# Seven products in place of eight for the last group of a feed-forward layer, on one Trainium2 core

## The reference

```
h2 = _rmsnorm(x, norm_mlp[l])
x = x + jnp.square(jax.nn.relu(h2 @ w_ff1[l])) @ w_ff2[l]
```

## Time and profile before

| | |
|---|---|
| median of 3 runs | 730.05 us |
| the profiled execution | 729.97 us |
| its span, first to last instruction | 728.2 us |
| PE busy | 722.0 us, 3460 matmuls |
| DVE busy | 520.8 us |
| ACT busy | 336.8 us |
| POOL busy | 241.6 us |

### The profile page before, as it was taken

The page is one execution under the profiler, slowest core; times in us unless marked ns, Lnnn a source line. Parts: engine busy times, 40 slices in busy tenths (PEclk is TensorE's granted clock), DMA queues, the critical chain, the costliest instruction groups (busy, mean ns, idle before and its releaser), DMA issues.

```text
span 728.2 us, 9745 instructions
## 1 busy us (share of the span) xinstructions
PE 722.0 (99%) x3460; PEld 576.6 (79%) x3460; DVE 520.8 (72%) x754; ACT 336.8 (46%) x483; POOL 241.6 (33%) x197
## 2 busy tenths in 40 slices
PE   8999999999999999999999999999999999999998
PEld 5878878787776666788889988888888888888887
DVE  6355887899886865537656569695968778695972
ACT  6244753465567777722334353534344252535320
POOL 4005225011224653003301091815436180816610
PEclk9999999999999999999999999999999999999999
DMA  9409231311111202133190225151331505131102
GB/s 322 149 15 264 83 117 58 116 58 58 58 58 30 74 16 57 59 116 115 38 338 3 75 98 175 59 173 58 116 115 51 179 0 177 53 115 58 58 16 101
DMA packets 44037, 70.62 MB, mean 97 GB/s; under 512 B 2657, under 2 KB 27489, under 8 KB 44002
## 3 DMA queue, kind: packets, MB, share of 16 engines
q1 hardware_dynamic: 44000, 70.16, 29.5%
q10 hardware_dynamic: 2, 0.00, 0.0%
HBM read 65.71 MB, written 2.10 MB: 93 GB/s over the span
## 4 chain that ended last, share of the span: by engine, by line
PE 94%; DVE 3%; ACT 1%; POOL 1%; issue 1%; DMA 0%; DVEq 0%; ACTq 0%
PE ps L1804 8%; PE ps L1803 8%; PE ps L1802 8%; PE ps L421 7%; PE ps L423 7%; PE ps L422 7%; PE ps L1830 6%; PE ps L1832 6%; PE ps L1831 6%; PE ps L414 6%; PE ps L416 5%; PE ps L415 5%; PE ps L1684 1%; PE ps L1620 1%; PE ps L1654 1%; PE ps L1716 1%
## 5 line engine op out<-in xcount | busy, mean ns | idle before, releaser
L1802 PE MATMUL ps<-b_hi,cut_hi 128*128 128x512 f32 (+1 forms) x280 | 104.1, 372 | 0.0
L1803 PE MATMUL ps<-b_lo,cut_hi 128*128 128x512 f32 (+1 forms) x280 | 103.9, 371 | 0.0
L1804 PE MATMUL ps<-b_hi,cut_lo 128*128 128x512 f32 (+1 forms) x280 | 103.9, 371 | 0.0
L421 PE MATMUL ps<-cut_hi,a_hi 128*128 128x512 f32 x224 | 90.3, 403 | 0.0
L423 PE MATMUL ps<-cut_hi,a_lo 128*128 128x512 f32 x224 | 87.7, 392 | 0.0
L422 PE MATMUL ps<-cut_lo,a_hi 128*128 128x512 f32 x224 | 87.6, 391 | 0.0
L909 ACT ACTIVATE qo_sb<-ps 128x512 f32<-128x512 f32 x32 | 19.2, 599 | 135.7 <-PE ps L1804 91.0
L631 POOL TENSOR_TENSOR a_lo<-qo_sb,a_hi 128x512 fp32r<-128x512 f32 x49 | 78.2, 1617 | 5.6 <-ACT a_hi L919 5.6
L405 DVE TENSOR_TENSOR cut_lo<-raw,cut_hi 128x2048 fp32r<-128x2048 f32 (+2 forms) x33 | 52.1, 1579 | 27.9 <-ACT cut_hi L397 27.9
L397 ACT ACTIVATE cut_hi<-raw 128x2048 fp32r<-128x2048 f32 (+2 forms) x33 | 48.5, 1468 | 31.1 <-PE ps L416 22.7
L1803 PEld LDWEIGHTS ps<-b_lo,cut_hi 128*128 128x128 f32 x280 | 52.8, 188 | 9.1
(11 more groups left out here) (199 smaller groups left out, 1665.7 us busy)
## 6 DMA issues: line engine op xcount, KB each, us to landing
raw<-in_w_ff_dram SPq DMA_DIRECT2D x32, 1024.0 KB, 5.6
raw<-in_w_in_dram SPq DMA_DIRECT2D x16, 1024.0 KB, 5.7
gates<-in_x_dram SPq DMA_DIRECT2D x8, 512.0 KB, 5.9
raw<-in_w_out_dram SPq DMA_DIRECT2D x4, 1024.0 KB, 5.0
raw<-in_w_in_dram SPq DMA_DIRECT2D x4, 512.0 KB, 7.4
raw<-in_w_branch_sb_dram SPq DMA_DIRECT2D x2, 1024.0 KB, 5.1
raw<-in_w_branch_sa_dram SPq DMA_DIRECT2D x4, 512.0 KB, 6.2
out_dram<-gates SPq DMA_DIRECT2D x7, 256.0 KB, 2.0
```

The source lines that it names most:

```text
L421: nc.tensor.matmul(dst, l_hi, w_hi, start=start, stop=False)
L1802: T.matmul(dst, w_hi[:, w], b_hi[:, k, a:b], start=(k == 0), stop=False)
L1803: T.matmul(dst, w_hi[:, w], b_lo[:, k, a:b], start=False, stop=False)
L1804: mm = T.matmul(dst, w_lo[:, w], b_hi[:, k, a:b], start=False, stop=(k == KD - 1))
```

## The change

Group 7 gets the seven products as well. The last full round (round 6) and group 7 are written out: PE takes the four first-product tiles of group 7 sooner, in the order tile 0, A11, S2, tile 1, A12, tile 2, S1, tile 3, S3, S4, A22; then the products of group 7 as A11, S2, S1, A12, S3, S4, A22. The second token tile of the last A22 is done in two halves of 256 columns, the second half in bank 6, and S3's part of it is added by itself. ACT, DVE and POOL get new lists to match (`act_last_end`, `dve_late`, `dve_last`, `left_parts_last`); DVE takes the first weights' second half remainder ahead of the first square. SP sends nine output parts out as `drain` finishes them.

```diff
+PE_TURN = {FG - 2: [A11, S2, A12, S1, S3, S4, A22], FG - 1: [A11, S2, S1, A12, S3, S4, A22]}
+LEFT_TURN = {FG - 1: [A11, A12, S2, S1, S3, S4, A22]}
+RIGHT_TURN = {FG - 1: PE_TURN[FG - 1]}
+OUT_PARTS = [(A12, 0, 0), (A12, 1, 0), (S3, 0, 0), (S3, 1, 0), (S4, 0, 0), (S4, 1, 0), (A22, 0, 0),
+             (A22, 1, 0), (A22, 1, 1)]
...
+        late_home = {(FG - 2, A22): home4[0], (FG - 1, A11): home4[1], (FG - 1, S2): home3[1], (FG - 1, S1): home4[2],
+                     (FG - 1, A12): home4[3], (FG - 1, S3): home3[0], (FG - 1, S4): home3[2], (FG - 1, A22): home4[0]}
...
-                sp.wait_ge(x_final, v + 1)
+                sp.wait_ge(drained, prod_end(FG - 1, q) - 1 + t + hf)
...
-            for c in range(4):
-                pool.wait_ge(hid_hi, c + 1)
-                pool.tensor_tensor(left_lo[:, c], pair(hid[:, c, :]), left_hi[:, c].bitcast(F32), ALU.subtract).then_inc(hid_lo, 1)
+            def left_parts_last(g):
+                pool.wait_ge(l_lo, 7 * g)
+                pool.wait_ge(s_made, 4 * g)
+                pool.wait_ge(f1_sq, 4 * g + 3)
+                left_low(g, A11)
+                pool.tensor_tensor(sum_of[S3], h11, h21, ALU.subtract).then_inc(s_made, 1)
+                pool.wait_ge(f1_sq, 4 * g + 4)
+                pool.tensor_tensor(sum_of[S1], h21, h22, ALU.add).then_inc(s_made, 1)
+                pool.wait_ge(s_made, 4 * g + 2)
+                pool.tensor_tensor(sum_of[S2], sum_of[S1], h11, ALU.subtract).then_inc(s_made, 1)
+                left_low(g, A12)
+                left_low(g, S2)
+                left_low(g, S1)
+                pool.wait_ge(s_made, 4 * g + 3)
+                pool.tensor_tensor(sum_of[S4], h12, sum_of[S2], ALU.subtract).then_inc(s_made, 1)
+                for q in (S3, S4, A22):
+                    left_low(g, q)
...
             def act_last_end(g):
-                last_high(0)
-                hidden_high(1)
                 right_high(g, S3)
+                right_high(g, A22)
+                right_high(g + 1, A11)
                 relu(g + 1, 2)
-                last_high(1)
-                last_high(2)
-                hidden_high(2)
-                right_high(g, A22)
-                last_high(3)
+                left_high(g + 1, A11)
+                right_high(g + 1, S2)
                 relu(g + 1, 3)
-                hidden_high(3)
+                right_high(g + 1, S1)
+                for q in (A12, S1, S2):
+                    left_high(g + 1, q)
+                right_high(g + 1, A12)
+                left_high(g + 1, S3)
+                right_high(g + 1, S3)
+                right_high(g + 1, S4)
+                left_high(g + 1, S4)
+                left_high(g + 1, A22)
+                right_high(g + 1, A22)
...
+                        if last and q == S3 and t == 1:
+                            dve.wait_ge(z_added, 6)
+                            half = xres[:, 3, 256:512]
+                            V.tensor_tensor(half, src[:, 256:512], half, ALU.add)
+                        if last and q == A22 and t == 1:
+                            V.tensor_tensor(part[:, 0:256], src[:, 0:256], part[:, 0:256], ALU.add).then_inc(drained, 1)
+                            dve.wait_ge(prod_done, prod_end(g, q) + 1)
+                            dve.wait_ge(drained, prod_end(g, S3))
+                            src, part = bank(6, 256, 512), part[:, 256:512]
...
+            def dve_late(g):
+                right_low(g, S2)
+                right_low(g, A12)
+                f_low(g + 1, 1)
+                square(g + 1, 0)
+                drain(g, A11)
+                drain(g, S2)
+                right_low(g, S1)
+                t4_made(g)
+                right_low(g, S4)
+                square(g + 1, 1)
+                drain(g, A12)
+                right_low(g, S3)
+                right_low(g, A22)
+                t1_made(g + 1)
+                right_low(g + 1, A11)
+                square(g + 1, 2)
+                t3_made(g + 1)
+                t2_made(g + 1)
+                drain(g, S1)
+                right_low(g + 1, S2)
+                square(g + 1, 3)
+                drain(g, S3)
+                right_low(g + 1, S1)
+                drain(g, S4)
+                right_low(g + 1, A12)
+                t4_made(g + 1)
+                right_low(g + 1, S3)
+                drain(g, A22)
+                right_low(g + 1, S4)
+            def dve_last(g):
+                drain(g, A11)
+                right_low(g, A22)
+                drain(g, S2)
+                add_z(S1)
+                drain(g, S1, last=True)
+                add_z(S4)
+                drain(g, A12)
+                add_z(A22)
+                drain(g, S3, last=True)
+                drain(g, S4, last=True)
+                drain(g, A22, last=True)
...
-            with pe.Fori(1, FG - 1) as g:
+            with pe.Fori(1, FG - 2) as g:
                 pe_round(g)
...
+            g = FG - 2
+            ff1(g + 1, 0)
+            product(g, A11)
+            product(g, S2)
+            ff1(g + 1, 1)
+            product(g, A12)
+            ff1(g + 1, 2)
+            product(g, S1)
+            ff1(g + 1, 3)
+            for q in (S3, S4, A22):
+                product(g, q)
+            for q in PE_TURN[g + 1]:
+                product(g + 1, q, halves=(q == A22))
```

More of the change, by code:

```diff
@@ L62, with place @@
 HI = [A11, A12, S1, S2, S3, S4, A22]
-LAST_BANK = [0, 1, 4, 5, 6, 7, 2, 3, 0]
-OUT_PARTS = [(u % TB, 512 * (u // TB), 512 * (u // TB) + 512) for u in range(7)] + [(3, 512, 768), (3, 768, 1024)]
+PE_TURN = {FG - 2: [A11, S2, A12, S1, S3, S4, A22], FG - 1: [A11, S2, S1, A12, S3, S4, A22]}
+LEFT_TURN = {FG - 1: [A11, A12, S2, S1, S3, S4, A22]}
+RIGHT_TURN = {FG - 1: PE_TURN[FG - 1]}
+def place(turns, g, q):
+    return turns[g].index(q) if isinstance(g, int) and g in turns else q
+OUT_PARTS = [(A12, 0, 0), (A12, 1, 0), (S3, 0, 0), (S3, 1, 0), (S4, 0, 0), (S4, 1, 0), (A22, 0, 0),
+             (A22, 1, 0), (A22, 1, 1)]
+PART = {A12: (0, 0), S1: (2, 1), S4: (0, 1), S3: (2, 1), A22: (2, 0)}
 ZCOL = [0, 512, 1024, 896]
@@ L381, in prod_end @@
         def prod_end(g, q):
[L383 removed]
+            return 14 * g + 2 * place(PE_TURN, g, q) + 2
         def cut_slot(i, part, k, nk):
@@ L932, in right_high @@
                     act.wait_ge(f1_done, 2)
+                elif isinstance(g, int) and (g, q) in ((FG - 2, A22), (FG - 1, A11)):
+                    act.wait_ge(f1_done, 4 * (FG - 1) + 2)
+                elif isinstance(g, int) and (g, q) in ((FG - 1, S1), (FG - 1, A12)):
+                    act.wait_ge(f1_done, 4 * (FG - 1) + 4)
+                elif isinstance(g, int) and g == FG - 1:
+                    act.wait_ge(prod_done, prod_end(FG - 2, {S2: S1, S3: S3, S4: S4, A22: A22}[q]))
                 elif not (first and q == S2):
@@ L1379, in drain @@
                     dve.wait_ge(prod_done, prod_end(g, q) - 1 + t)
-                    if last and q == A22:
-                        dve.wait_ge(z_added, 4 + t + 1)
+                    if last and q in Z_TURN:
+                        dve.wait_ge(z_added, 2 * Z_TURN.index(q) + t + 1)
                     elif not (first and back):
-                        dve.wait_ge(drained, 14 * (g + back) + 2 * wrote + t + 1)
+                        dve.wait_ge(drained, prod_end(g + back, wrote) - 1 + t)
                     src = bank(BANK[q] + t)
@@ L1825, in product @@
                     if not (first and back):
[L1826 to L1833, removed]
+                        pe.wait_ge(drained, prod_end(g + back, before) - 1 + t)
+                    for a, b in ((0, 256), (256, S)) if halves and t else ((0, S),):
+                        for j in range(2):
+                            l_h, l_l = (part[:, q, j, t * P:(t + 1) * P] for part in (left_hi, left_lo))
+                            dst = bank(6 if a else BANK[q] + t, a, b)
+                            T.matmul(dst, l_h, hi[:, j, a:b], start=(opens or a > 0) and j == 0, stop=False, skip_group_check=True)
+                            T.matmul(dst, l_h, lo[:, j, a:b], start=False, stop=False, skip_group_check=True)
+                            mm = T.matmul(dst, l_l, hi[:, j, a:b], start=False, stop=(j == 1), skip_group_check=True)
+                        mm.then_inc(prod_done, 1)
             pe.wait_ge(f_lo, 1)
@@ L1864, in _ @@
             pe_round(0, first=True)
-            with pe.Fori(1, FG - 1) as g:
+            with pe.Fori(1, FG - 2) as g:
                 pe_round(g)
[L1867 to L1887, removed]
-                mm.then_inc(last_done, 1)
+            g = FG - 2
[11 more added lines that the diff above has]
+                product(g + 1, q, halves=(q == A22))
 _INS = ["x", "norm_mix", "w_in", "q_norm_sb", "k_norm_sb", "q_norm_sa", "k_norm_sa",
```

90 lines of the change are left out of this document (30 added, 60 removed).

## The result

The changed kernel takes 731.76 us (median of 11 executions, 730.76 to 732.46); the kernel before took 730.05 beside it (11 executions, 729.76 to 730.27). The ratio is 1.0022, with a 95% interval of 1.0014 to 1.0031: slower by 1.71 us, 0.23%. That lies inside the predicted range and 0.26 us beyond the border of 731.5 between "same" and "slower"; the interval, 0.14% to 0.31%, reaches to both sides of that border (0.2%).

What follows compares the result with a forecast made beforehand. The prediction took PE's number of matmuls to bound the end. Its terms, -2.80 (matmuls) + 3.76 (stall) + 0 (outputs) = +0.96 us, on 729.97 profiled, plus 0.08 for the median, gave 731.0 us, range 728.8 to 732.9.

Steps and rivals of the forecast that it cites:

- border of 731.5: Whole kernel: 728.6 and 731.5 us bound "same"; chances were faster 0.19, same 0.51, slower 0.30.
- Part 1: PE's matmuls of group 7: 19.12 us instead of 21.92, 2.80 us less on the path.
- the relu of tile 1: Round 6: it waits for POOL's last remainder of group 6, forecast to end at 683.4 instead of 680.27.
- Part 2: Work added off PE: DVE's late A22 drain stalls PE ahead of product S2 of group 7, costing 3.76 us.
- I count four times 1.0 to 1.2: DVE's waits for POOL between 698.4 and 709.2: four, 4.45 us in all, with none to five possible.
- the sign of being right: PE gapless from 662.78 to 706.3, then one idle time of 3 to 4 us ahead of group 7's S2.
- No further wait arises: After the stall PE's banks are drained in time, 0.7 us ahead at the closest (S3 before A22).
- Part 3: ACT copies, weight load and nine closer outputs at no price: 0, up to +0.5 or -0.3 us for outputs.
- The estimate of 380 GB/s: Full output transfer rate, giving 0.7 us per 256 KB; the last 128 KB finds the queue just empty.
- rival D: Something late and unseen, such as PE's longer straight program or a slow output queue: +1 to +2 us; chance 0.03.
- Rival B: No PE stall ahead of S2 of group 7, as DVE's A22 drain comes earlier: 727.3 us; chance 0.17.
- Rival C: The stall drops PE's clock to 1.2 GHz for 3.7 us, costing 1.8 us: 732.8 us; chance 0.10.

Runs made afterwards that it cites:

- e2: The changed kernel with POOL's four sums and seven remainders of group 7 cut to 32 of 256 columns: 727.10 us.
- e4: The changed kernel with every other output transfer issued by ACT instead of SP: 731.70 us.
- e1: The changed kernel with DVE's drains of A22 of round 6 moved ahead of T4 and the remainder of S3: 730.74 us.
- e9: e5 with 200 already fulfilled waits spread over PE's program of round 6: 727.77 us.
- e10: The changed kernel with 200 already fulfilled waits in PE's program of round 6 and nothing else: 730.06 us.
- e3: The changed kernel without its first four output transfers (A12 and S3): 729.87 us.
- e6: e5 with the drain of A22 of round 6 late again, behind the remainder of S3: 732.16 us.
- e8: e5 with every other output issued by ACT: 728.93 us.
- e5: The changed kernel with six zsum additions moved from DVE to POOL, the early A22 drain of e1 and DVE's last list reordered: 729.06 us.
- e7: e1 with every other output issued by ACT: 730.83 us.

## Why the prediction was right or wrong

The time (731.0 against 731.76) and the place of the stall were right, but the middle of the sum was right only because two wrong terms nearly cancel, the stall 1.20 us too long and the outputs 1.56 too short: that is luck. And the median lies by a hair beyond the border to "slower", where "same" was the likeliest.

- **Part 1, -2.80 us: right.** e2 gives 2.80 to the hundredth. Round 6 stayed gapless in its new order; the relu of tile 1, forecast at 683.4 for POOL's last remainder, came at 683.76 with 0.34 of it the shifted start. That order wasn't tried by itself.
- **Part 2, the stall: place, releaser and mechanism right; its size, 3.76, was 1.2 too much.** The term that failed is "I count four times 1.0 to 1.2", with the reason that like rows "hold one full turn per instruction". Three turns were lost, not four, so that PE's idle time was 2.33 us, below the 3 to 4 given as the sign of being right. DVE was behind its S4 drains (PSUM, not held by POOL) at 702.71, and POOL's operation, let go at about 701.5, needs 1.25 us, thus until about 702.75, by this working: who comes first was a matter of 0.05 us, and the remainder of A12 went first, in 1.21. In e4 another remainder, that of A22, took 2.34 us where after has 1.21. Rows can show that turns are taken, not who gets each one; the range for this (none to five) held, the point estimate deserved less weight.
- **"No further wait arises": right for after,** with a margin given as 0.7 us. e1 shows how thin it was: with the first wait cured the gap stands at that very bank, 1.64 us.
- **Part 3, outputs, "0" with a bound of +0.5: wrong, +1.56.** The estimate of 380 GB/s was right (376 GB/s from 726 to 728), and so was the queue just emptying, but for something that isn't an output: the fetch of PE's longer straight program. The prediction named "the longer straight PE program" only in rival D, at 0.03; D's price, +1 to +2, is what came. The packet was to be seen in the trace of before, in the queue of instructions at 700 to 702; I read the outputs' queue and not that one. e9 and e10 put its price at 1.5 us each.
- **Rival B, no stall, 727.3:** what e2 (727.10) gets by shortening POOL's work, so its price was right and its condition wasn't met.
- **Rival C, the clock: 0.10 was too low.** The profiled execution of after doesn't have it, but five of 11 of e10 and four of e3 do, at about 1.4 us against 1.8 priced. The ground given against it, that an idle time of 2.4 us stood in the trace of before and the granted clock was 1.00, didn't carry: that one lies at the start, and a gap of 2.33 us was enough in e6. The Trainium skill's rule (TensorE: Matmul & The Clock Gate, "Part 1: The HAM clock gate") that idleness halves the clock agrees in those executions: 0.50 in e6. Behind the same gap after's profile has 1.00.

The sum with the measured terms: -2.80 + 2.56 + 1.56 = +1.32; the remaining 0.4 is mostly the 0.34 by which the common point lies later in that execution.

Open: whether SP's issue stands still because the engine that carries the packet can't take its share of the next output is argued from their times, not shown; in e8 no issue was long and one engine was late nevertheless. The Trainium skill (DMA: Bandwidth & Descriptors, "🔬 Queues, rings and completion order") says that a DMA engine drains a whole packet of one queue before it turns to another; that would fit if the 16 KB are one packet in that sense, which no run here shows. With no output in flight the packet takes 0.97 to 1.30 us (before, e3, e9, e10), among outputs 0.94 to 1.89: why it takes 0.94 in e2 and does no harm there, and 1.86 in after, isn't explained either.

## What to carry to other kernels

Saving matmuls on a PE-bound stretch moves work to DVE and POOL: count the operations of two SBUF operands on both in that same stretch, and give each up to twice its time, before the saving is booked. Put a drain where the next bank is needed, but if the engine's list is full, that only moves the wait (e1); with six additions fewer on DVE and another order it was gone (e5, which doesn't part the two). And when a kernel ends in a bunch of small outputs, look where the instruction packets fall: a longer straight program can put one among them, and moving it cost nothing that could be measured here (e9, e10).

## What the runs showed that I had not expected

- A program packet of 16 KB among full output transfers: up to 1.89 us on one DMA engine (e7), an output issue of 1.71 to 2.24 us in place of 0.33 (e1, after, e6, e5), the end 1.5 us later (e9, e10).
- 200 waits for counts already reached, put between PE's matmuls, cost nothing that can be seen: e9 and e10 reach the last addition as e5 and after do, within 0.04 us.
- Behind one and the same idle time of 2.33 us the granted clock was 1.00 in one execution (after) and about 0.50 for 3 us in another (e6).
- Where two engines take turns, a small shift, by the working above 0.05 us, decides over 1.1: 1.21 or 2.34 us for one instruction (after, e4).
